# Differential attention: xq, q and k of heads 4-7 computed by tokens and turned, memory heads first, heads 0-3 last

## What is computed

```
proj = h @ w_in                                  # 1024 -> 1024 q, 1024 k, 1024 v, 512 xq
q, k: 8 heads x 2 components x 64;  v: 8 heads x 128;  xq: 4 memory heads x 128
s = q @ k.T / 8 - slope[head] * distance, causal  # per head and component
w = softmax(s[:, 0]) - lam * softmax(s[:, 1])
o = rmsnorm(w @ v, norm_g) * (1 - lam_init)      # per head
xo = softmax(xq @ mem_k.T / sqrt(128)) @ mem_v   # memory heads, 256 memory rows
out = concat([o, xo]) @ w_out                    # 12 tiles of 128 features -> 1024
```

## Time and profile before

| | |
|---|---|
| median of 3 runs | 1419.28 us (1418.56 to 1419.42) |
| profiled execution | 1418.27 us, its span 1416.5 us |
| TensorE | 1403.6 us busy, 99% |
| VectorE, ScalarE, GpSimd | 857.3 us (61%), 704.9 us (50%), 259.8 us (18%) |
| granted TensorE clock | 0.999, so 2.4 GHz |
| DMA | 275.55 MB, mean 195 GB/s |
| the stage in question | 683.65 to about 824 us of the span |

### The profile page before, as it was taken

How to read it: one execution, slowest core, us unless ns; L and a number is a source line. 1 busy time by engine, 2 the same in 40 slices (tenths; PEclk the granted TensorE clock), 3 DMA queues, 4 the chain that set the end, 5 groups by cost and what they waited for, 6 DMA issues and landing times.

```text
span 1416.5 us, 18653 instructions
## 1 busy us (share of the span) xinstructions
PE 1403.6 (99%) x7200; PEld 1190.3 (84%) x7200; DVE 857.3 (61%) x1035; ACT 704.9 (50%) x981; POOL 259.8 (18%) x504
## 2 busy tenths in 40 slices
PE   9999999999999999999999999999999999999998
PEld 7888889988888888888889888888887989888886
DVE  5656565756555565555656565555796655565554
ACT  6554454445444454444555555444555554644443
POOL 1022210002222222222012113222201100132222
PEclk9999999999999999999999999999999999999999
DMA  9765654455655656665544446665553553366562
GB/s 349 290 213 201 219 186 156 166 185 192 221 201 198 218 196 215 207 220 198 180 149 150 139 168 258 216 222 200 186 177 136 188 179 134 125 228 225 197 220 74
DMA packets 71655, 275.55 MB, mean 195 GB/s; under 512 B 17392, under 2 KB 37232, under 8 KB 40848
## 3 DMA queue, kind: packets, MB, share of 16 engines
q1 hardware_dynamic: 57168, 259.57, 51.6%
q0 software_dynamic: 14400, 14.81, 3.4%
HBM read 259.88 MB, written 1.05 MB: 184 GB/s over the span
## 4 chain that ended last, share of the span: by engine, by line
PE 95%; ACT 2%; DVE 1%; issue 1%; DMA 0%; POOL 0%; SPq 0%; DVEq 0%; POOLq 0%; ACTq 0%
PE prod L1140 16%; PE prod L1141 16%; PE prod L1144 15%; PE acc L1144 10%; PE acc L1140 10%; PE acc L1141 10%; PE prod L1134 5%; PE prod L1136 5%; PE prod L1135 5%; PE acc L1338 1%; PE acc L1159 1%; ACT w_hi L1493 1%; PE acc L1358 1%; DVE w_lo L1743 0%; PE o_bank L1394 0%
## 5 line engine op out<-in xcount | busy, mean ns | idle before, releaser
L1743 DVE TENSOR_TENSOR w_lo<-raw,w_hi 128x2048 fp32r<-128x2048 f32 x233 | 533.6, 2291 | 383.4 <-ACT w_hi L1493 380.8
L1493 ACT CAST w_hi<-raw 128x2048 fp32r<-128x2048 f32 x233 | 444.2, 1907 | 431.6 <-PE prod L1144 182.1
L1140 PE MATMUL prod<-w_hi,acts_h 128*128 128x512 f32 x944 | 370.2, 392 | 2.5 <-DVE w_lo L1752 1.8
L1144 PE MATMUL prod<-w_hi,acts_l 128*128 128x512 f32 x944 | 367.7, 389 | 0.0
L1141 PE MATMUL prod<-w_lo,acts_h 128*128 128x512 f32 x944 | 367.4, 389 | 0.0
L1004 POOL DMA_DIRECT2D four<-four x408 | 200.1, 498 | 602.4 <-DVE four L1904 585.3
L1140 PE MATMUL acc<-w_hi,mix_h 128*128 128x512 f32 x600 | 236.0, 393 | 0.0
L1144 PE MATMUL acc<-w_hi,mix_l 128*128 128x512 f32 x600 | 233.7, 390 | 0.0
L1141 PE MATMUL acc<-w_lo,mix_h 128*128 128x512 f32 x600 | 233.5, 389 | 0.0
L1140 PEld LDWEIGHTS prod<-w_hi,acts_h 128*128 128x128 f32 x944 | 177.2, 188 | 43.0 <-issue 6.9
L1144 PEld LDWEIGHTS prod<-w_hi,acts_l 128*128 128x128 f32 x944 | 177.2, 188 | 37.5 <-DVE acts_l L1814 0.3
(11 more groups left out here) (277 smaller groups left out, 1261.7 us busy)
## 6 DMA issues: line engine op xcount, KB each, us to landing
raw<-in_weights_dram SPq DMA_DIRECT2D x234, 1024.0 KB, 5.0
four<-four SPq DMA_DIRECT2D x408, 16.0 KB, 2.1
four<-four POOLq DMA_DIRECT2D x408, 16.0 KB, 1.9
raw<-in_weights_dram SPq DMA_DIRECT2D x16, 256.0 KB, 6.9
work<-in_mem_dram POOLq DMA_DIRECT2D x2, 1024.0 KB, 13.5
grow<-in_gain_rows_dram POOLq DMA_DIRECT2D x4, 512.0 KB, 3.7
tabs<-in_tabs_dram POOLq DMA_DIRECT2D x1, 1632.0 KB, 9.9
work<-in_x_t_dram SPq DMA_DIRECT2D x4, 256.0 KB, 5.7
```

Source lines behind the costliest of these rows:

```text
L1140: pe.matmul(out, still_hi, wh, start=first, stop=False, skip_group_check=True)
L1144: return pe.matmul(out, still_lo, wh, start=False, stop=last, skip_group_check=True)
L1493: act.copy(w_hi[:, c % RING], raw[:, c % RAW]).then_inc(hi_done, 1)
L1743: dve.tensor_tensor(w_lo[:, c % RING], raw[:, c % RAW], w_hi[:, c % RING].bitcast(F32), ALU.subtract).then_inc(lo_done, 1)
```

## The change

In the plan of the differential stage:

- `project_turned` is new: token-wise chunks as in `project_tokens`, then ScalarE writes the result by tokens into a buffer in cut order (scaled by the token's root mean square, times a factor per head for q: the item `scales`, computed by POOL), VectorE transposes all 1024 columns of it in 32 x 32 blocks, and 16 transfers of 32 KB (8 by SP behind a weight load, 8 by POOL) move the blocks to their partitions.
- xq, q of heads 4-7 and k of heads 4-7 are computed so, with two chunks each, instead of with two feature-wise chunks each. Heads 0-3 stay feature-wise.
- The result lies with a step of eight words between tokens (`in_tokens`), and the scores of these heads read it so: q and k of heads 4-7, q of the memory heads.
- The order is: xq; then memory heads' scores while q, k and v of heads 4-7 are computed; heads 4-7; q, k of pair 0, v of heads 0-3, q, k of pair 1; heads 0-3, of which 2 and 3 get their scores in the drain. `spread` comes just before the first feature-wise chunk. The output projection takes tiles by pairs 4, 5, 2, 3, 0, 1. `hold_turn` isn't used.
- ScalarE waits for the moves before a later value readout and before the next `prep`.

In the second block the first `mem_prep` of the second memory moves into the drain of `w_out_2`, behind its first chunk, before `open` of the second and head 3's `head_scale`.

```diff
+    def project_turned(self, source, col, dest, at, buffers, of="x", mid=None, between=None, scales=None):
+        for k_half in range(2):
+            self.chunk("rows_half", (*source, "half", (k_half, col)), mid, e=self.e, k_half=k_half, dest=dest, at=at,
+                       of=of, acts=self.acts if of == "x" else self.mem, free=self.bank_free(2), turned=self.turned,
+                       buffers=buffers, scales=scales)
+            self.used(of)
+            if between and k_half == 0:
+                between()
+        self.turn_behind[self.c + RAW] = self.items[-1]
+        self.turned += 1
+        for t in range(2):
+            self.bank_reader.append(("cut_done", 2 * self.turned - 1 + t))
+        self.e += 2
...
-    memory = mem_units(4, P, "xq", 1)
+    memory = mem_units(4, P, "xq", 1, q_blocks=True)
...
-                     rows=None, v=("v", h * P), out="norm") for h in range(HEADS)]
-    norms = HeadNorms(pl, heads, "diff")
-    ticks = pl.ticks([[unit] for unit in heads + memory])
+                     rows=None, v=("v", h * P), out="norm", q_blocks=h >= 4, k_blocks=h >= 4) for h in range(HEADS)]
+    heads_in_order = heads[4:8] + heads[0:4]
+    norms = HeadNorms(pl, heads_in_order, "diff")
+    ticks = pl.ticks([[unit] for unit in memory + heads_in_order])
...
-    query(0, None)
+    pl.project_turned(w, 3 * D, "xq", 0, "diff", scales=pl.scales([P ** -0.5]))
+    pl.ready(memory)
+    pl.ready_v(memory)
+    pl.project_turned(w, 512, "q", 4, "diff",
+                      scales=pl.scales([2.0 ** (h + 1) * 64 ** -0.5 for h in range(4, 8)]))
+    end(slot)
+    pl.project_turned(w, D + 512, "k", 4, "diff", mid=slot, between=lambda: end(slot))
+    end(slot)
+    pl.project_tokens(w, 2 * D + 512, "v", 512, mid=slot, between=lambda: end(slot))
+    pl.ready(heads[4:8])
+    pl.ready_v(heads[4:8])
+    end(slot)
     pl.spread("x")
...
-    downs(slot, "diff_w_out", 0, pairs_of(0, 1, 2, 4, 5, 3), memory_turned)
+    downs(slot, "diff_w_out", 0, pairs_of(4, 5, 2, 3, 0, 1))
...
-    pl.mem_prep("g_mem", [4, 5, 6, 7], [8, 9, 10, 11], "mem2")
...
     downs(slot, "w_out_2", 0, order,
-          lambda n: n == 1 and pl.mem_prep("g_mem", [0, 1, 2, 3], [4, 5, 6, 7], "mem2"))
+          lambda n: n < 2 and pl.mem_prep("g_mem", *(([4, 5, 6, 7], [8, 9, 10, 11]), ([0, 1, 2, 3], [4, 5, 6, 7]))[n],
+                                          "mem2"))
...
+        def in_tokens(name, tile):
+            four_tiles = dests[name][:, tile // 4 * 4:tile // 4 * 4 + 4].rearrange("p a b -> p (a b)")
+            return four_tiles.rearrange("p (i t k) -> p k t i", t=2, k=4)[:, tile % 4]
...
+                if c in plan.turn_behind:
+                    move_features(sp, plan.turn_behind[c], (0, 1), early_features_moved)
...
+                    if unit["moved"]:
+                        pe.wait_ge(early_features_moved, 128 * unit["moved"])
+                        pe.wait_ge(late_features_moved, 128 * unit["moved"])
...
+                        if it["turned"]:
+                            act.wait_ge(features_turned, it["turned"])
...
+                        dve.wait_ge(cut_done, 2 * it["turned"] + 2)
+                        if it["turned"]:
+                            dve.wait_ge(early_features_moved, 128 * it["turned"])
+                            dve.wait_ge(late_features_moved, 128 * it["turned"])
+                        dve.transpose(cut_buffer(it, 1).rearrange("p (b i n) -> p b n i", b=4, n=8),
+                                      cut_buffer(it, 0).rearrange("p (b n j) -> p b n j", b=4, n=8)
+                                      ).then_inc(features_turned, 1)
```

More of the change, by code:

```diff
@@ L218, in prep @@
                       x_new=self.x_new, y=self.y, y_chunk=self.y_chunk, x_turned=self.x_turned, n=self.stat,
-                      double=double, wait=wait)
+                      double=double, wait=wait, moved=self.turned)
         if last_down is not None:
@@ L337, in project_tokens, with scales @@
             self.e += 2
+    def project_turned(self, source, col, dest, at, buffers, of="x", mid=None, between=None, scales=None):
[11 more added lines that the diff above has]
+        self.e += 2
+    def scales(self, factors):
+        at = self.n_scales
+        self.n_scales += len(factors)
+        self.add("scales", factors=factors, at=at, stat=self.stat)
+        return list(range(at, at + len(factors)))
     def ticks(self, groups):
@@ L416, in ready @@
         for unit in units:
-            unit["need"], unit["rope"] = self.read, self.rope_n
+            unit["need"], unit["rope"], unit["moved"] = self.read, self.rope_n, self.turned
     def ready_v(self, units):
@@ L474, in early @@
         if self.scales >= 2 * (self.turns + 1) and not self.hold_turn:
-            self.pl.head_turn(self.turns, self.which)
+            self.pl.head_turn(self.units[2 * self.turns]["head"] // 2, self.which)
             self.turns += 1
@@ L479, in late @@
         if self.splits < self.turns:
-            self.pl.head_lo(self.splits, self.which)
+            self.pl.head_lo(self.units[2 * self.splits]["head"] // 2, self.which)
             self.splits += 1
@@ L616, in value @@
         pl.ready_v(heads[2 * pair:2 * pair + 4])
-    query(0, None)
-    pl.spread("x")
[L620 to L629, removed]
+    pl.project_turned(w, 3 * D, "xq", 0, "diff", scales=pl.scales([P ** -0.5]))
[10 more added lines that the diff above has]
+    end(slot)
+    pl.spread("x")
+    for pair in range(2):
         query(pair)
@@ L634, in make_plan @@
         pl.ready(heads[2 * pair:2 * pair + 2])
[L635 to L639, removed]
-    pl.draining = True
[L641 to L645, removed]
-    downs(slot, "diff_w_out", 0, pairs_of(0, 1, 2, 4, 5, 3), memory_turned)
+        if pair == 0:
+            value(0)
+    pl.draining = True
+    downs(slot, "diff_w_out", 0, pairs_of(4, 5, 2, 3, 0, 1))
     pl.draining = False
@@ L1100, in _ @@
                     move_blocks(pool, (2, 3), late_blocks_moved)
+                elif kind == "rows_half" and it["k_half"] and it.get("turned") is not None:
+                    move_features(pool, it, (2, 3), late_features_moved)
+                elif kind == "scales":
+                    pool.wait_ge(rstd_done, it["stat"])
+                    for n, factor in enumerate(it["factors"]):
+                        ins = pool.tensor_scalar(scales[:, 2 * (it["at"] + n):2 * (it["at"] + n) + 2], rstd["x"], factor,
+                                                 None, ALU.mult)
+                    ins.then_inc(scales_done, len(it["factors"]))
                 elif kind == "load_mem2":
@@ L1605, in _ @@
                     flush(state["target"] - 1)
+                    if it["moved"] and it["resid"] != "post":
+                        act.wait_ge(early_features_moved, 128 * it["moved"])
+                        act.wait_ge(late_features_moved, 128 * it["moved"])
                     act.wait_ge(chunk_used, it["acts_free"])
```

76 lines of the change are left out of this document (68 added, 8 removed).

## The result

The changed kernel took 1427.46 us (median of 4 runs, 1426.96 to 1429.06) where the kernel before took 1419.35 (4 runs, 1418.56 to 1419.45) beside it: 8.1 us more, ratio 1.0061, 95% interval 1.0045 to 1.0077. The profiled execution has a span of 1425.8 us against 1416.5, 9.3 more. The forecast was 1418.2, no change that can be told; the range ended at 1422.6. It was wrong.

What follows compares the result with a forecast made beforehand. TensorE, busy 99% of the span, was taken as the bound: its streaming plus few gaps. Terms -1.6 - 1.3 + 0.2 + 0.9 + 0.2 + 0 + 0.5 = -1.1 us gave 1418.2 from median 1419.28; range 1415.6 to 1422.6.

Steps and rivals of the forecast that it cites:

- part 3: Readouts of the stage's turned chunks: hidden except before memory head 2's output, +0.2 us, from 0 to +1.3.
- part 5: Scores of heads 4-7 and memory heads' queries read with a 32-byte step: 0 taken, at most +6.8 us.
- part 4: Head order in the stage: components scored singly in the drain +0.9 us, more slots +0.2, end 0 to +1.
- Part 1: Six stage chunks go from feature-wise to token-wise, 5.84 to 5.57 us each: -1.6 us.
- Part 2: Stage's slow opening (-0.4) and PE's wait on the values' readout (-0.9) go: -1.3 us, bounds 0 to -1.3.
- the singles: Heads 2 and 3 scored one component at a time in the drain, 0.65 us each: +0.9 us, 0 if overlapped.
- first rival: Strided reads cost in scores of heads 4-7 and memory heads: +6.8 us, giving 1425.0; chance 0.13.
- the upper bound: Each strided score record of heads 4-7 and memory heads doubles, expected under the cacheline rule: +6.8 us.
- Part 6: Second block's mem_prep moved into w_out_2's drain: -1.0 before, +1.5 there, together +0.5 us, from -1.0 to +0.8.
- 0.2 for more slots: In the stage, 27 instead of 25 slots interrupt PE's stream, about 0.1 us each: +0.2 us.
- Strided reads are dear: Strided scores of heads 4-7 and memory heads cost +6.8 us, ending slower at 1425.0; chance 0.13.
- half-priced first rival: Strided scores of heads 4-7 and memory heads at half their dear price, given as the range's upper end, 1422.6 us.

Runs made afterwards that it cites:

- experiment 5: Changed kernel with one more POOL transfer, keys of heads 4-7 turned in runs of 32 words, and mem_prep back at its old place: 1419.72 us, ratio 1.0008.
- experiment 9: Kernel before with only the change's order; xq, queries and keys of heads 4-7 feature-wise, mem_prep at its old place: 1419.96 us, ratio 1.0009.
- experiment 4: Changed kernel with keys of heads 4-7 turned into runs of 32 words, queries still strided: 1425.95 us, ratio 1.0052.
- experiment 7: Kernel before with only the second block's mem_prep moved into the drain of w_out_2: 1418.76 us, ratio 1.0003.
- experiment 1: Changed kernel with one more transfer on POOL's queue, behind the third turned group's moves: 1421.58 us, ratio 1.0021.
- experiment 3: Kernel before with 24 more POOL transfers of 32 rows each at the start of the stage: 1424.98 us, ratio 1.0043.
- experiment 8: Kernel before with 24 more POOL transfers of one row each at the start of the stage: 1425.33 us, one run.
- experiment 2: Changed kernel with one more POOL memset, of a pad nothing reads, behind the third turned group's moves: 1428.12 us, ratio 1.0065.
- experiment 6: As experiment 5, but queries of heads 4-7 feature-wise again and nine pad transfers on POOL instead of one: 1419.04 us, ratio 1.0004.

## Why the prediction was wrong

Three steps of it failed. POOL's 24 added transfers were costed at nothing beyond the stage (part 3), and they were worth +6.1 us. Reads with a step were put at 0 (part 5), and they cost +3.4 and +0.2. A single component in the drain was put at 0.65 us (part 4), and it takes 0.84. The gains were forecast about right.

**Part 1, six chunks token-wise (-1.6): right as far as can be told.** In the changed stage their matmuls start 0.23 us apart, 24 to a chunk, where 48 started 0.12 apart. No run has the form without another change of its own, so the term is not isolated. The passes of the whole stage took 2.35 us less; parts 1 and 2 forecast 2.9, and the late bank of part 3 (0.3) and the losses beside single components (0.4, part 4) stand against it.

**Part 2, stalls that go (-1.3): right.** The 0.72 us wait on the values' readout and the slow opening are gone.

**Part 3, readouts within the stage (+0.2): right there, wrong outside.** The turns took 2.2 us, the upper of the two values and not the 1.25 that I took; with the output in runs they do take 1.25 (experiment 5). The price was 0.3 us before memory head 2's output, for the 0.2 taken, and none elsewhere. What failed is a half sentence: POOL's 24 transfers were costed by what they delay inside the stage, and nothing by what they do to the numbers of the transfers behind it. That one line was worth +6.1 of the 9.3 us. It could have been asked before: POOL's group in the earlier trace rows has 16.9 us of idle time that ends in "issue", 15.3 of it at one spot, the turn at 470 us, where its moves start 3.4 us after the turn for no reason that the trace names (the other 1.6 lie in the middle of one turn's moves, at 1351 us). There the lateness cost PE nothing, so I hadn't followed it. A stall without a releaser is one whose place I can't predict, and it should have widened the range.

**Part 4, order (+1.1, of it +0.9 for the singles): mis-sized.** One component alone takes 0.84 us, not 0.65. Its records start 0.21, 0.11 and 0.22 us apart and the next instruction 0.31 behind the last, where I had 0.108, 0.108, 0.215 and 0.215. The pair of the earlier trace rows has the same steps for both of its components together, so its 0.85 already held the excess, and two singles pay it twice. The excess stands where records on 64 rows border on ones on 128, whatever these are, transposes or passes; the memory heads, on 128 rows, don't have it. Outside the 0.84 the neighbours lose as much: the pass before a single is followed by it after 0.32 us in place of 0.23, and the instruction behind it by the next after 0.1 us more. So heads 2 and 3 cost +1.7 in their scores and another 4 x 0.2 - 2 x 0.2 = 0.4 beside them, which is what experiment 9 showed over its 0.9. Pair 1 at the end was in time, as forecast.

**Part 5, reads with a step (0, at most +6.8): the wrong end.** It was this part's first rival, at half its size. I argued that a read at half speed would still feed an fp32 record; the runs say no. A head with both operands strided takes 1.70, with the stationary one alone 1.26, with none 0.86: 0.44 for the moving operand, 0.40 for the stationary one, +3.4 over four heads. (The moving operand's step was never run without the other.) The memory heads, whose stationary operand alone is strided, pay less: their four records start 0.220, 0.238 and 0.239 us apart where experiment 9, at the same places with contiguous queries, has 0.220, 0.215 and 0.215, and with the step behind the last it is 0.07 a head; the first head loses 0.1 more at the next passes, and nothing here shows why. The weight loads (PEld) show where the stationary share comes from. Heads of the stage before, then heads 4-7 and the memory heads of the changed kernel, busy us and mean ns:

```profile
L1338 PEld LDWEIGHTS acc<-work 64*128 64x128 f32 x64 | 4.2, 186 | 1.8 <-issue 1.2
L1415 PEld LDWEIGHTS acc<-work 64*128 64x128 f32 x32 | 4.1, 327 | 1.0 <-issue 0.7
L1415 PEld LDWEIGHTS acc<-mem_k,obuf 128*128 128x128 f32 x16 | 4.1, 328 | 0.2
```

A strided load takes 0.33 us instead of 0.19 in both, and 0.33 in experiment 4 as well, where the keys lie in runs. A memory head's records start 0.215 us apart, and the longer load is nearly covered; a component has records only 0.11 apart, and there it isn't. That this is why the same load costs 0.40 in one place and 0.07 in the other fits the rows, and no run isolates it. By the Trainium skill, "Advanced Engine Details and Errata", section SBUF Cachelines, a different 16-byte line at each access brings a performance penalty; this case's traces agree for heads 4-7, where the pair doubled, and hardly for the memory heads. The rule gives no size and doesn't tell the operands apart, so "the upper bound" that the prediction drew from it was its own reading.

**Part 6, mem_prep (+0.5): right.** One wait of 0.9 gone, one of 1.2 come; net 0.3, and experiment 7 shows it without the rest.

**The sum again** with the measured terms where there are any: -1.6 - 1.3 + 0.3 + 1.7 + 0.2 + 3.4 + 0.2 = +2.9 for the stage, as the traces show. The agreement is partly luck: the -1.6 and the 0.2 for more slots are the forecast's, and the 0.4 beside the singles has no term. With +0.3 for mem_prep, +6.1 in the FFN, and the +0.3 and -0.3 of the table that no part explains, it is 9.3, the difference of the spans. The medians lie 8.1 us apart.

**The range and the rivals.** "Strided reads are dear" named 1425.0 and would have been 1421.8 by itself. None named a stall behind the stage. The range's upper end was called the half-priced first rival; by its own terms that is 1418.2 + 3.4 = 1421.6, not 1422.6. Experiment 1, the changed kernel without the stall, took 1421.6 and lies inside the range, but not for the forecast's reasons: strided reads and single components make up the difference to 1418.2.

What stays open: why the 134th and the 262nd transfer on POOL's queue start late. A period of 128 is not shown beyond two instances: the 390th starts without a stop in the kernel before, and its stop of 0.5 us in the changed one is at the 391st in experiment 1, so it keeps its place and not its number. The same holds for a longer stop that the traces do not explain either, in the middle of the moves behind one turn near the end: 1.6 us before the 392nd in the kernel before, 1.5 before the 416th in the changed one, and 1.5 before the 417th in experiment 1. So not every late transfer of POOL is a matter of its number. And half of the length of the FFN's stall is argued, not tested by a run of its own: that the weight loads, once ahead, hold up the last moves is read from the packets by stretch alone.

## What to carry to other kernels

An added transfer on POOL's queue is paid not only where it stands: it renumbers every later one. If a trace shows a start that is late for no releaser, count which transfer of the queue it is, and put one that nobody waits for at that number. And a strided fp32 operand is not free because matmuls look slow: look at the loads' mean time too. Where a turn can write runs of 32 words instead, its own time falls from 2.2 to 1.25 us as well.

A wait of some 4 us of PE costs more than itself; add the stretch at half the clock behind it, here 2.4 us on 3.8.

## What the runs showed of the hardware

- The 134th transfer on POOL's queue started 3.4 us after the turn that releases it in all ten experiments and both kernels, and the 262nd 1.6 to 2.4 us behind the end of its predecessor, or 2.83 us after its turn, in nine kernels in which its start is free of other waits; moves behind other turns start 0.3 us after them. It is the count of transfers, whether of 1 or 32 rows (experiments 3 and 8), and one more memset changed nothing (experiment 2).
- POOL's moves of 16 KB, once behind two 1 MB loads of SP, got no packet through from 849.9 to 852 us, while the loads held 94% of the engines (changed kernel).
- A stream turn of 1024 columns takes 1.25 us with the output in runs (experiment 5) and 2.2 with a step of 8 words (changed kernel).
- A 32-byte step costs a pair of 64-row components 0.40 us in the stationary operand and 0.44 us more in the moving one, on 0.86; a pattern of four runs of 32 words in the moving operand costs nothing (experiments 4 and 6). A load of the strided stationary operand takes 0.33 us instead of 0.19.
- Going from fp32 or fp32r records on 128 rows to fp32 records on 64 rows costs 0.2 us, and going back as much (both kernels and experiment 9); fp32 records on 128 rows among fp32r passes show no such loss (memory heads of experiment 9).
- After a stand of 3.8 us the granted clock was 0.50 for 5.2 us of full work, then 1.00 again (changed kernel).
